# The last gate chunk of a feed-forward half and the split of the next weight block: a change of order on two engines

## The chip, the cores and the metric

One NeuronCore of one Trainium2 chip runs the whole program. The time is device microseconds (us) of one execution, as the median of the runs. TensorE (PE) multiplies, VectorE (DVE) and ScalarE (ACT) do everything elementwise, GpSimd (POOL) computes a few roots, and SyncE's queue (SP) starts the weight transfers.

## What is computed

Two transformer layers with adaptive normalization (feed-forward, a mixer, feed-forward each), then two hybrid layers and a final norm, on a context of 256 rows and a sequence of 256 rows, width 1024. The change concerns the feed-forward sublayers alone, of which there are four: ffn00, ffn01, ffn10 and ffn11 (layer, which of the two). The first three work on 512 columns (context and sequence), ffn11 on the 256 of the sequence alone, since nothing reads the context afterwards.

```python
D_MODEL = 1024; D_FF = 2816

def _ffn_sublayer(h, mod, g_pre, g_post, w_in, w_out):
    shift, scale, gate = mod
    u = _modulate(_rmsnorm(h, g_pre), shift, scale)
    a, b = jnp.split(u @ w_in, 2, axis=-1)
    y = (jax.nn.silu(a) * b) @ w_out
    return h + MACARON_W * gate * _rmsnorm(y, g_post)
```

## The kernel before, in words

Activations lie transposed: 128 features on the partitions, columns of the sequence along the free axis. Every large product is made of fp32 operands that are split in two parts of reduced precision, high and low, so that one step over 128 features is three matmuls: high by high, high by low, low by high (`product_step`, L915 to L917). Each operand therefore has two tiles: `uR` (normalized input) and `gR` (gated hidden values) with their parts 0 and 1, and the weights `wh` and `wl`.

**Weights.** They come as blocks of 128 x 2048 values or less, in two slots. SP starts a block's transfer into `wraw` as soon as the block two before it has been split (it waits for the semaphore `w_lo`, L671). ACT rounds the block into `wh` (`lead`, L1602), DVE subtracts to get `wl` (`rest`, L2096, or in two halves L2114) and then raises `w_lo`, which PE waits for at the start of the block. `lead` also waits until PE has done with the slot's old block. So the split of a block runs while PE works on the block before it.

**A feed-forward sublayer** is cut in two halves of the hidden width: 12 chunks of 128 and then 10. In each half a loop (two chunks to a turn) makes the gate chunks: PE makes a chunk's two products, a and b; ACT takes the silu of a (L1912) into `half`; DVE multiplies it by b (L2639); ACT then copies the product as `gR` high (L1916); DVE subtracts for `gR` low (L2644) and raises `g_ready`. After the loop comes the output projection of the half (`out_proj`): 8 weight blocks (`out0` to `out7` in this text), one for each 128 output features, each multiplied with all 12 (or 10) chunks of `gR`. The very first of them starts right after the last gate product, and waits for `g_ready` chunk by chunk, so only its last step needs the last gate chunk.

**Order of the work on ACT and DVE**, before. For each gate chunk ACT does: silu, `lead` of the block two ahead, copy to `gR` high. DVE does: multiply, `rest` of that block, subtract for `gR` low. The blocks two ahead of the last two gate blocks are out0 and out1. Each engine takes its instructions strictly in the order written; `do` also makes it wait for its own instruction before it signals others (the idle time that such a signal ends is listed as DVEq L2002 or ACTq L1542). In the first half's projection ACT copies each of the 8 products out of PSUM (L1922) and then leads the next block. In the second half DVE adds the products to `yT` (L2668), and the pieces of the norm that follows run beside it.

**Between sublayers.** The function `residual` ends a sublayer on DVE with a chain: variance, root on POOL (L1963), spread over the partitions by PE (L866), scaling, adding, normalizing (L2191, L2196, L2072, L2081). The next sublayer's block 1 is split inside this chain in two column halves (`rest_part`, L2114): the first half before the last wait for POOL's root (signal `w_half`), since PE's first step makes three products together, two of block 0 and the first of block 1. The second half and its `w_lo` come after the whole chain, except ahead of the sublayer na, where both halves stand in front.

**ada chunks.** ffn00, ffn01 and the second half of ffn10 carry a side product, one to a turn: PE L820, copied by ACT to `gs` (L1564, `ada_out`), then turned by PE (L830, `ada_turn`). In the loops the turn comes a turn later; after the loop of ffn10's second half PE does the last one at once, ahead of the output projection.

## Time and profile before

| | us |
|---|---|
| median of three runs | 2489.59 (2488.76, 2489.59, 2499.67) |
| the profiled execution, its own time | 2494.8 |
| its span, first to last instruction | 2492.9 |
| PE busy | 2341.6 (94%) |
| DVE busy | 1239.6 (50%) |
| ACT busy | 1022.9 (41%) |
| POOL busy | 33.5 (1%) |
| mean granted clock of TensorE | 0.968 |

PE is the engine that is nearly always busy. The time that a change of order can move is PE's idle time, so the rows to look for are those in which PE waits: each carries in brackets how long it had been idle and which engine's signal ended the idle time. PE's rows overlap, since matmuls are pipelined; the distance between two starts is the pace.

### The profile page before, as it was taken

What the parts mean: (1) busy time and instruction counts of PE and PEld (TensorE: products, weight loads), DVE (VectorE), ACT (ScalarE), POOL (GpSimd) and SP (SyncE); (2) the same over time, 40 slices, a digit from 0 to 9 for tenths busy, and PEclk for the clock granted to TensorE, in tenths of its full rate; (3) what the DMA queues carried; (4) which work ended last, traced back from release to release, by engine and by line L of the source; (5) the groups of instructions that cost most, each with busy time, mean ns of one, the idle gap of its engine ahead of it and who ended that gap; (6) DMA issues with size and microseconds to landing.
All of it is one profiled execution on the core that took longest, in us unless ns stands there. A gap on an engine that the chain in (4) does not pass through costs nothing.

```text
span 2492.9 us, 41414 instructions
## 1 busy us (share of the span) xinstructions
PE 2341.6 (94%) x15342; PEld 2007.9 (81%) x15342; DVE 1239.6 (50%) x1709; ACT 1022.9 (41%) x1459; POOL 33.5 (1%) x35
## 2 busy tenths in 40 slices
PE   6999999899898999998999999899789979998998
PEld 5888888777677888887888877777689979988997
DVE  4332335755656322337432336655564576856765
ACT  4332224543455332235322224543554455344543
POOL 0000000000000000000000000000000000000000
PEclk8999999999999999999999999999999999999999
DMA  9553553322214544542333643422245543214221
GB/s 305 186 177 93 170 175 94 114 90 85 85 35 135 157 142 139 168 131 72 103 87 106 193 138 95 113 79 69 68 135 169 160 139 112 69 54 138 85 69 52
DMA packets 396899, 298.16 MB, mean 120 GB/s; under 512 B 10846, under 2 KB 358756, under 8 KB 396644
## 3 DMA queue, kind: packets, MB, share of 16 engines
q1 hardware_dynamic: 363274, 231.12, 31.2%
q10 hardware_dynamic: 33498, 65.35, 7.3%
q8 instruction: 80, 1.31, 0.2%
q14 instruction: 47, 0.39, 0.1%
HBM read 295.38 MB, written 1.06 MB: 119 GB/s over the span
## 4 chain that ended last, share of the span: by engine, by line
PE 80%; DVE 10%; ACT 4%; issue 3%; DMA 1%; SPq 1%; DVEq 0%; POOL 0%; ACTq 0%; POOLq 0%
PE banks L915 23%; PE banks L916 22%; PE banks L917 22%; DVE wl L2096 3%; PE banks L1173 3%; PE banks L820 2%; ACT wh L1602 2%; DVE wl L2114 1%; PE banks L1024 1%; SPq L671 1%; PE banks L1045 1%; DMA scratch<-in_ada_w 1%; PE banks L1131 1%; PE banks L1031 0%; PE banks L1221 0%
## 5 line engine op out<-in xcount | busy, mean ns | idle before, releaser
L915 PE MATMUL banks<-uR,wh 128*128 128x512 f32 (+2 forms) x2368 | 835.7, 353 | 41.7 <-DVE uR L2081 25.7
L916 PE MATMUL banks<-uR,wh 128*128 128x512 f32 (+2 forms) x2368 | 821.2, 347 | 0.0
L917 PE MATMUL banks<-uR,wl 128*128 128x512 f32 (+2 forms) x2368 | 819.7, 346 | 0.0
L2096 DVE TENSOR_TENSOR wl<-wraw,wh 128x2048 fp32r<-128x2048 f32 (+2 forms) x214 | 453.1, 2117 | 428.0 <-ACTq L1542 423.2
L1602 ACT ACTIVATE wh<-wraw 128x2048 fp32r<-128x2048 f32 (+2 forms) x224 | 398.7, 1780 | 482.6 <-PE banks L917 450.7
L915 PEld LDWEIGHTS banks<-uR,wh 128*128 128x128 f32 (+1 forms) x2368 | 458.8, 194 | 105.0 <-issue 41.3
L917 PEld LDWEIGHTS banks<-uR,wl 128*128 128x128 f32 (+1 forms) x2368 | 458.1, 193 | 52.9
L916 PEld LDWEIGHTS banks<-uR,wh 128*128 128x128 f32 (+1 forms) x2368 | 458.8, 194 | 49.7 <-issue 0.5
L915 PE MATMUL banks<-gR,wh 128*128 128x512 f32 (+1 forms) x704 | 256.5, 364 | 4.6 <-DVEq L2002 4.5
L916 PE MATMUL banks<-gR,wh 128*128 128x512 f32 (+1 forms) x704 | 255.4, 363 | 0.0
L917 PE MATMUL banks<-gR,wl 128*128 128x512 f32 (+1 forms) x704 | 255.3, 363 | 0.0
L2639 DVE TENSOR_TENSOR half<-half,banks 128x512 f32<-128x512 f32 (+1 forms) x88 | 54.7, 622 | 400.7 <-PE banks L917 390.2
L915 PEld LDWEIGHTS banks<-gR,wh 128*128 128x128 f32 x704 | 132.9, 189 | 27.4 <-DVEq L2002 3.7
L917 PEld LDWEIGHTS banks<-gR,wl 128*128 128x128 f32 x704 | 132.9, 189 | 20.6
L916 PEld LDWEIGHTS banks<-gR,wh 128*128 128x128 f32 x704 | 132.9, 189 | 20.2
L1912 ACT ACTIVATE half<-banks 128x512 f32<-128x512 f32 (+1 forms) x88 | 47.9, 545 | 169.0 <-PE banks L917 140.6
L915 PE MATMUL banks<-wh,uR 128*128 128x256 f32 (+1 forms) x320 | 93.2, 291 | 2.2 <-DVEq L2002 2.2
L917 PE MATMUL banks<-wh,uR 128*128 128x256 f32 (+1 forms) x320 | 90.5, 283 | 0.0
L916 PE MATMUL banks<-wl,uR 128*128 128x256 f32 (+1 forms) x320 | 90.5, 283 | 0.0
L1922 ACT ACTIVATE yT<-banks 128x512 f32<-128x512 f32 (+1 forms) x32 | 17.4, 545 | 159.6 <-PE banks L917 159.6
L1593 ACT ACTIVATE uR<-yT,mod,coefA 128x256 fp32r<-128x256 f32 x88 | 52.2, 594 | 56.4 <-DVE yT L2072 56.3
L2644 DVE TENSOR_TENSOR gR<-half,gR 128x512 f32 (+1 forms) x88 | 55.1, 626 | 30.5 <-DVE wl L2096 30.5
(305 smaller groups left out, 2398.0 us busy)
## 6 DMA issues: line engine op xcount, KB each, us to landing
wraw<-in_ffn_w_in SPq DMA_DIRECT2D x176, 512.0 KB, 5.0
ada_buf<-in_ada_w ACTq DMA_DIRECT2D x27, 2048.0 KB, 8.3
wraw<-in_w_in SPq DMA_DIRECT2D x56, 512.0 KB, 4.5
wraw<-in_ffn_w_out SPq DMA_DIRECT2D x64, 384.0 KB, 4.1
wraw<-in_ffn_w_out SPq DMA_DIRECT2D x64, 320.0 KB, 3.7
wraw<-in_da_w_in SPq DMA_DIRECT2D x24, 512.0 KB, 4.5
wraw<-in_na_w_in SPq DMA_DIRECT2D x24, 512.0 KB, 4.4
yT<-in_ada_w ACTq DMA_DIRECT2D x4, 2048.0 KB, 8.4
```

What stands on the lines that cost most here:

```text
L671: sp.dma_start(dst, src).then_inc(w_in[s], 16)
L820: ins = mm(o[32 * j:32 * j + 32, 0:P], sc[:, k, :], w[:, k, j * P:j * P + P], start=(k == 0), stop=(k == DC - 1))
L915: mm(o, a[0], b[0], start=first, stop=False)
L916: mm(o, a[0], b[1], start=False, stop=False)
L917: return mm(o, a[1], b[0], start=False, stop=last)
L1173: ins = mm(o[:, h * P:h * P + P], a, b, start=(k == 0), stop=(k == len(parts) - 1))
L1593: A_(uR[:, 0, k, a], yT[:, k, a], ACT.Identity, **at_)
L1602: do(A_(wh[:, s, 0:n], wraw[:, s, 0:n], ACT.Copy), w_hi)
L1912: do(A_(half[:, s, 0:w], o[:, 0:w], ACT.Silu), silu_ready)
L2096: do(V.tensor_tensor(wl[:, s, 0:n], wraw[:, s, 0:n], wh[:, s, 0:n].bitcast(F32), ALU.subtract), w_lo)
L2639: do(V.tensor_tensor(half[:, s, 0:w], half[:, s, 0:w], o[:, 0:w], ALU.mult), free_a, free_b, gm_ready)
L2644: do(V.tensor_tensor(gR[:, 1, k, c0:T], half[:, s:s + 1, 0:w], gR[:, 0, k, c0:T].bitcast(F32), ALU.subtract), g_ready)
```

## The change

Three edits, all on ACT and DVE:

1. The last turn of each gate loop is written out after the loop, and in its second chunk, the last of the half, the `gR` work stands before the weight work: on ACT the copy, then `lead`; on DVE the subtraction for `gR` low, then `rest`. The block is out1 of the half. All other chunks keep their order. This concerns 8 places.
2. In the first half's output projection ACT leads the next block before it copies the product out of PSUM (32 places).
3. Ahead of ffn11, `residual` splits the second column half of block 1 right after the first, ahead of the wait for the root, and no longer after the chain.

```diff
@@ ScalarE
+                        def two_chunks(i, last):
                             ada_load(carries, n0, i)
                             for s in range(2):
...
-                                lead(s)
+                                if not (last and s):
+                                    lead(s)
                                 act.wait_ge(gm_ready, tl["gm"].up())
                                 do(A_(gR[:, 0, bass.ds(i * 2 + s, 1), c0:T], half[:, s:s + 1, 0:w], ACT.Copy), gh_ready)
+                                if last and s:
+                                    lead(s)
                             if carries:
                                 ada_out()
+
+                        with repeat(act, kc // 2 - 1, (gemm, 4), (own, 6 + len(ada)), (tl["g"], 2), (tl["gm"], 2), (tl["w0"], 32),
+                                    (tl["w1"], 32), (tl["split"], 2), *ada) as i:
+                            two_chunks(i, False)
+                        two_chunks(kc // 2 - 1, True)
                         if part == 0:
                             for b in range(DC):
                                 o, free = product()
+                                lead_next()
                                 do(A_(yT[:, b:b + 1, c0:T], o[:, 0:w].rearrange(one, a=1), ACT.Copy), free)
-                                lead_next()
@@ VectorE, residual
-                if to not in SUB or to == "na":
+                if to not in SUB or to in ("na", "ffn11"):
                     rest_part(b, 1, to in SUB, w_lo)
...
-                if to in SUB and to != "na":
+                if to in SUB and to not in ("na", "ffn11"):
                     rest_part(b, 1, True, w_lo)
@@ VectorE, gate chunks
-                                rest(s)
+                                if not (last and s):
+                                    rest(s)
                                 dve.wait_ge(gh_ready, tl["gh"].up())
                                 k = bass.ds(i * 2 + s, 1)
                                 do(V.tensor_tensor(gR[:, 1, k, c0:T], half[:, s:s + 1, 0:w],
                                                    gR[:, 0, k, c0:T].bitcast(F32), ALU.subtract), g_ready)
+                                if last and s:
+                                    rest(s)
```

ACT at the end of ffn11's first gate loop and the start of its output projection, before (L156 is the loop's end, L1916 the copy to `gR` high, L1602 the lead, first of out1, then of out2):

```order
L1912 ACTIVATE half<-banks 128x256
L1540 REGISTER_ALU
L1599 REGISTER_ALU
L1602 ACTIVATE wh<-wraw 128x2048
L1540 REGISTER_ALU
L1916 ISA
L1916 ACTIVATE gR<-half 128x256
L1540 REGISTER_ALU
L156 REGISTER_ALU
L156 COMPARE_AND_BRANCH
L1922 ACTIVATE yT<-banks 128x256
L1602 ACTIVATE wh<-wraw 128x1536
```

The same place after the change, from the silu of the loop's last chunk on (L1917 is now the copy to `gR` high, L1931 the copy out of PSUM):

```order
L1912 ACTIVATE half<-banks 128x256
L1917 ACTIVATE gR<-half 128x256
L1602 ACTIVATE wh<-wraw 128x2048
L1602 ACTIVATE wh<-wraw 128x1536
L1931 ACTIVATE yT<-banks 128x256
L1602 ACTIVATE wh<-wraw 128x1536
```

The copy of the last chunk has moved ahead of the 2048-wide lead, and each projection's lead ahead of its copy; DVE is reordered in the same manner (subtraction L2653, then L2104).

DVE ahead of ffn11, before: the end of the variance chain, the first column half of block 1, and the start of scaling.

```order
L2178 TENSOR_SCALAR stat<-stat 128x2
L2114 TENSOR_TENSOR wl<-wraw,wh 128x8x128
L2030 CAST rootR<-stat 128x2
L2031 TENSOR_TENSOR rootR<-stat,rootR 128x2
L2191 TENSOR_TENSOR yT<-yT,banks 128x256 x2
L2196 TENSOR_TENSOR hT<-hT,yT 128x256
```

The same place after the change:

```order
L2186 TENSOR_SCALAR stat<-stat 128x2
L2122 TENSOR_TENSOR wl<-wraw,wh 128x8x128 x2
L2038 CAST rootR<-stat 128x2
L2039 TENSOR_TENSOR rootR<-stat,rootR 128x2
L2199 TENSOR_TENSOR yT<-yT,banks 128x256 x2
L2204 TENSOR_TENSOR hT<-hT,yT 128x256
```

Two column halves now stand ahead of the cast that waits for the root, where one stood; the one behind the chain is gone.

ACT at the end of ffn10's second gate loop after the change (L1564 is `ada_out`, for which PE's turn L830 waits):

```order
L1912 ACTIVATE half<-banks 128x512
L1917 ACTIVATE gR<-half 128x512
L1602 ACTIVATE wh<-wraw 128x2048
L1564 ACTIVATE gs<-banks 128x128
L1602 ACTIVATE wh<-wraw 128x1280
L1937 ACTIVATE scratch<-yT 128x512
```

Before, the lead stood ahead of the copy; `ada_out` was and is behind both. PE's and SP's instructions are the same, in the same order, in both kernels.

## Rows read from the trace of the kernel before

**Rows 1.** The page: the span, and PE's line of busy time.

```profile
span 2492.9 us, 41414 instructions
PE 2341.6 (94%) x15342; PEld 2007.9 (81%) x15342; DVE 1239.6 (50%) x1709; ACT 1022.9 (41%) x1459; POOL 33.5 (1%) x35
```

**Rows 2.** Waits, 1805 to 2060 us: line, releaser: us in total, times, longest.

```profile
PE banks L915 <- DVEq L2002: 9.3, 5, 2.9
```

**Rows 3.** Timeline, ffn11, end of first half's gates: start, duration, instruction, [idle before <-releaser].

```profile
1888.71 1.92 ACT L1602 ACTIVATE wh<-wraw 128x2048 fp32r<-128x2048 f32 x1 [2.42 <-PE banks L917]
1888.80 0.42 DVE L2639 TENSOR_TENSOR half<-half,banks 128x256 f32<-128x256 f32 x1 [0.67 <-PE banks L917]
1890.70 2.29 DVE L2096 TENSOR_TENSOR wl<-wraw,wh 128x2048 fp32r<-128x2048 f32 x1 [1.48 <-ACTq L1542]
...
1893.38 0.42 DVE L2644 TENSOR_TENSOR gR<-half,gR 128x256 f32 x1 [0.39 <-DVE wl L2096]
1892.35 0.28 PE L917 MATMUL banks<-gR,wl 128*128 128x256 f32 x1
1893.92 0.39 PE L915 MATMUL banks<-gR,wh 128*128 128x256 f32 x1 [1.29 <-DVEq L2002]
```

**Rows 4.** Timeline, ffn11's first gates, on DVE and ACT.

```profile
1831.84 0.42 DVE L2639 TENSOR_TENSOR half<-half,banks 128x256 f32<-128x256 f32 x1 [0.40 <-DVE gR L2644]
...
1832.65 0.42 ACT L1916 ACTIVATE gR<-half 128x256 f32 x1 [0.96 <-DVEq L2002]
```

**Rows 5.** Timeline, ffn11, output projection of the first half.

```profile
1912.55 1.49 ACT L1602 ACTIVATE wh<-wraw 128x1536 fp32r<-128x1536 f32 x1 [0.18 <-ACT yT L1922]
1922.30 1.92 ACT L1602 ACTIVATE wh<-wraw 128x2048 fp32r<-128x2048 f32 x1 [1.29 <-DMA wraw<-in_ffn_w_in]
1926.78 0.38 PE L915 MATMUL banks<-uR,wh 128*128 128x256 f32 x1 [1.87 <-DVEq L2002]
```

**Rows 6.** Timeline, ffn11, output projection of the second half.

```profile
1991.35 0.39 PE L915 MATMUL banks<-gR,wh 128*128 128x256 f32 x1 [2.01 <-DVEq L2002]
2000.76 1.27 ACT L1602 ACTIVATE wh<-wraw 128x1280 fp32r<-128x1280 f32 x1 [2.18 <-DMA wraw<-in_ffn_w_out]
2003.97 0.36 PE L915 MATMUL banks<-gR,wh 128*128 128x256 f32 x1 [1.21 <-DVEq L2002]
```

**Rows 7.** Timeline, from the chain ahead of ffn11 to its third weight block.

```profile
1808.60 0.70 POOL L1963 TENSOR_TENSOR stat<-stat,lams 128x2 f32<-128x2 f32 x1 [1.94 <-DVEq L2002]
1808.61 1.26 DVE L2114 TENSOR_TENSOR wl<-wraw,wh 128x1024 fp32r<-128x1024 f32 x1
1810.09 0.17 DVE L2030 CAST rootR<-stat 128x2 fp32r<-128x2 f32 x1 [0.22 <-DVE wl L2114]
1813.95 0.55 PE L915 MATMUL banks<-uR,wh 128*128 128x256 f32 x1 [2.27 <-DVE uR L2081]
1822.77 1.22 DVE L2114 TENSOR_TENSOR wl<-wraw,wh 128x1024 fp32r<-128x1024 f32 x1
1830.82 0.38 PE L915 MATMUL banks<-uR,wh 128*128 128x256 f32 x1 [2.93 <-DVEq L2002]
```

**Rows 8.** Timeline, ffn10, end of the first half's gates (512 columns).

```profile
1305.59 0.69 DVE L2639 TENSOR_TENSOR half<-half,banks 128x512 f32<-128x512 f32 x1 [5.61 <-PE banks L917]
...
1313.66 0.60 ACT L1922 ACTIVATE yT<-banks 128x512 f32<-128x512 f32 x1 [5.39 <-PE banks L917]
```

**Rows 9.** Timeline, ffn10, end of the second half's gates.

```profile
1488.80 0.69 DVE L2639 TENSOR_TENSOR half<-half,banks 128x512 f32<-128x512 f32 x1 [5.21 <-PE banks L917]
1491.72 0.28 ACT L1564 ACTIVATE gs<-banks 128x128 f32<-128x128 f32 x1 [0.25 <-ACT gR L1916]
1492.10 0.33 PE L830 MATMUL banks<-cst,gs 128*128 128x128 f32 x1 [1.54 <-ACTq L1542]
```

**Rows 10.** Stretches: us, busy (instructions) of PE, PEld, DVE, ACT, POOL, PEclk, DMA share, GB/s.

```profile
1900.00:1925.00 25.00, 24.91 (x207) 24.63 (x205) 9.50 (x6) 10.78 (x12) 0.00 (x0) 1.00 0.71 206
1928.00:1932.00 4.00, 4.00 (x23) 4.00 (x23) 2.29 (x1) 1.29 (x2) 0.00 (x0) 0.57 0.94 264
```

More of the change, by code:

```diff
@@ L1904, in _ @@
                         ada, n0 = [(tl["ada"], 1)] if carries else [], tl["ada"].n
-                        with repeat(act, kc // 2, (gemm, 4), (own, 6 + len(ada)), (tl["g"], 2), (tl["gm"], 2), (tl["w0"], 32),
-                                    (tl["w1"], 32), (tl["split"], 2), *ada) as i:
+                        def two_chunks(i, last):
                             ada_load(carries, n0, i)
@@ L2630, in _, with two_chunks @@
                         ada = [(tl["ada"], 1)] if ada_parts(st)[part] else []
-                        with repeat(dve, kc // 2, (gemm, 4), (own, 6 + len(ada)), (tl["silu"], 2), (tl["gh"], 2),
-                                    (tl["split"], 2), *ada) as i:
+                        def two_chunks(i, last):
                             for s in range(2):
@@ L2645, in _ @@
                                                    gR[:, 0, k, c0:T].bitcast(F32), ALU.subtract), g_ready)
+                                if last and s:
+                                    rest(s)
+                        with repeat(dve, kc // 2 - 1, (gemm, 4), (own, 6 + len(ada)), (tl["silu"], 2), (tl["gh"], 2),
+                                    (tl["split"], 2), *ada) as i:
+                            two_chunks(i, False)
+                        two_chunks(kc // 2 - 1, True)
                         if part == 0:
```

## The prediction

> **What bounds the kernel now.** I read the page first: PE is busy 94% of a span of 2492.9 us, DVE and ACT half of it [rows 1]. So only PE's idle time can be given back by a change of order, 2492.9 - 2341.6 = 151 us in all. Next came the waits of PE by stretch, and then the timeline at the places that the diff touches. In ffn11, from 1805 to 2060 us, PE waited for a signal of DVE before a product step five times, 9.3 us together [rows 2]. They are: 2.93 us for the third weight block [rows 7], 1.29 us for the last gate chunk of the first half [rows 3], 1.87 us for the first gate block of the second half [rows 5], 2.01 us for the last gate chunk of the second half and 1.21 us for a later block of that projection [rows 6]. In the three sublayers of 512 columns PE's steps last twice as long and the same places show no wait, but for one: the last turn of the ada product in ffn10, 1.54 us [rows 9].
>
> **Edit 1, the last gate chunk first, in ffn11's first half.** What goes: the wait for `g_ready`, 1.29 us. What comes is read off the same rows, with the instructions in their new order. The multiplication ends at 1888.80 + 0.42 = 1889.22 [rows 3]. Its signal took 0.39 us to start ACT's copy elsewhere (1832.26 to 1832.65 [rows 4]), so the copy runs from 1889.61 to 1890.03 (0.42). The lead follows an ACT copy by 0.18 us [rows 5]: 1890.21 to 1892.13 (1.92). DVE began its subtraction 0.07 us after the lead (1890.63 to 1890.70): 1892.20 to 1894.49 (2.29), and PE hears of DVE after 0.12 us (1893.80 to 1893.92): 1894.61 [all rows 3]. PE's pace is 25.00 / 207 = 0.12 us a matmul [rows 10]. Without the wait it runs on from 1892.35 for three more matmuls and wants out1 at 1892.83; before, it reached out1 at 1893.92 plus three, about 1894.38. So **the wait does not go, it moves by one step**: from `g_ready`, 1.29 us, to `w_lo` of out1, 1.8 us, and PE starts out1 at 1894.61 against 1894.38, +0.2 us. The 0.39 us holds the loop's register instructions, which the written-out turn doesn't have; halved, the result is 0. I take +0.1, bounds 0 and +0.4. The gain that the edit seems to promise is excluded: lead and subtraction alone need 4.2 us after 1890.03.
>
> **The same in the second half.** PE's wait was 2.01 us there and is about 2.5 us for out1 now, +0.1 us by the same steps. But DVE and ACT also take up the projection's next blocks earlier, since the lead of out2 no longer waits for PE. The later wait of 1.21 us hangs on a transfer that landed at 2000.76, after ACT had waited 2.18 us for it [rows 6]; the transfer starts when out2 is split. By the new order that is some 0.7 us earlier, while the transfer ahead of it (out3) starts 1.5 us later. After that DVE's chain is back to back to the end of the sublayer, so what is won there stays. Bounds: -1.2 (the wait goes) and +0.4 (the transfer is pushed back); I take -0.5 for the half, which is the 0.7 less half of the 0.4.
>
> **Edit 1 in the six wide halves.** The tightest is ffn10's first, which has no ada product between. The multiplication ends at 1306.28; then 0.39 signal, 0.60 copy (as L1922), 0.18, 1.92, 0.07, 2.29, 0.12: out1 is ready at 1311.85. PE wants it when out0 is done, about 0.2 us before ACT's copy of it at 1313.66 [rows 8]: 1.6 us of cover. The others have the ada product in between, about 2 us (PE's idle time before 1492.10 began at 1490.56, its last gate product ended near 1488.6 [rows 9]); the second halves' group is a sixth shorter, 1.4 us of 8.2. I cost them at 0; the work that hides them is PE's out0.
>
> **Edit 1 at ffn10's last turn.** PE turns the ada product right after the loop, behind ACT's `ada_out`, which is behind lead and copy. Before, lead, copy and `ada_out` began 0.09 us before the multiplication (as in rows 3), at 1488.71, and `ada_out` started at 1491.72, 3.01 us on. Now the copy has to wait for the multiplication, 1488.80 + 0.69 + 0.39 = 1489.88, and `ada_out` starts at 1492.89: the wait of 1.54 us becomes up to 2.7. With the shorter signal it is 1.0 more. **+1.0 us**, bounds +0.8 and +1.2.
>
> **Edit 2, lead before copy.** ACT's copy (0.38) and the gap behind it (0.18) leave the chain lead, subtraction, transfer [rows 5]: 0.56 us. Where PE bounds the blocks it is worth nothing, which is everywhere at 512 columns. It counts once: ffn11's first gate block of the second half, for whose transfer ACT waited 1.29 us and PE 1.87 us. The transfer starts when out6 is split, hence 0.56 us earlier. **-0.56 us**, bounds -1.2 and 0. Each PSUM bank is free 1.5 to 1.9 us later; its next user is four products on, so that costs nothing.
>
> **Edit 3, the second column half in front.** DVE's first half runs from 1808.61 to 1809.87; POOL's root was ready at 1809.30, and the cast that needs it started at 1810.09 with DVE as its releaser [rows 7]. DVE is the last to arrive, so a second half in front adds its whole length, 1.22 to 1.26 us, to the chain. Behind it are queued scaling, addition and normalization of all eight feature blocks, hence PE's first step of ffn11 (1813.95). What it takes away was hidden: at 1822.77 to 1823.99 PE was busy with its 72 first matmuls until after 1824.4. The 2.93 us wait that follows hangs on the third block, whose lead needs PE to be done with block 0, and stays. SP gets to load the fourth block earlier, which nobody awaits. **+1.24 us**, bounds 0 (if the root is the later one after all) and +1.3.
>
> Here a page speaks of the same place. POOL's root ran from 1808.60 to 1809.30, 0.70 us, together with DVE's half split, which took 1.26 us against 1.22 us without POOL [rows 7]; neither held the other up. The Trainium skill, "SBUF — State Buffer", section "Who interferes with whom", says that a DVE instruction with two SBUF inputs and a GpSimd instruction that reads SBUF exclude each other for their whole length. By that rule the root could be held until both halves are done; the rows speak against it.
>
> **The sum.** +0.1 - 0.5 + 1.0 - 0.56 + 1.24 = +1.3 us. On the profiled execution that is 2494.8 to 2496.1; it was 5 us above the median of the runs, and the difference applies as it is: 2489.59 + 1.3 = **2490.9 us**. This is no change: about 0.5%, 12 us, is what a measurement of this kernel can tell.
>
> **Rivals.**
>
> *The gains come without the costs* (17%). The root is late enough to hide edit 3, the wait of 1.21 goes whole, and the lower clock behind the 1.87 us wait goes with it: from 1928 to 1932 the granted clock was 0.57, that is mostly 1.2 GHz, and PE made 23 matmuls in 4 us, where the pace before gives 33 [rows 10], 1.2 to 1.7 us lost. 0.1 - 1.1 + 1.0 - 0.56 - 1.7 = -2.3: 2487.3.
>
> *Waits that grew bring the lower clock* (15%). The same row the other way: three waits are longer now, 2.6 us in ffn10 and 1.8 and 2.5 us in ffn11. Against it: after the wait of 1.29 us the clock was 1.00 from 1900 to 1925 [rows 10]. If each is followed by such a stretch: 1.3 + 3 x 1.5 = +5.8, 2495.4.
>
> *The cover is gone* (4%), the slower side. If out1 comes later than PE wants it in the wide halves too, each of eight loses what it is late. It decides at 1.6 us beyond the working above; with a transfer or a signal late by twice that, 8 x 1.6 = 13 us: 2503.
>
> *Root and split exclude each other* (4%). POOL would start after the second half, at 1811.1, and end 0.70 us later; the cast starts at 1812.0 and not 1811.3. +2.0: 2491.6. It is what the skill's page named above gives.
>
> *Nothing moves* (10%). The small terms cancel: 2489.6.
>
> **How the numbers follow.** The forecast has 50%, its own range 2489 to 2493. The range of 8 in 10 takes in the faster rival with its bound of edit 2, and the clock rival, and two to three us of the runs' own scatter on each side: 2485 to 2498. Faster by over 0.5%: 3%; only the cover's rival is slower by as much, with a stray median 5%; within: 92%.
>
> **What would show it.** Right: PE's wait for `g_ready` at the two ends of ffn11's gates gone, and a wait of 1.5 to 2.5 us 36 (or 30) matmuls after the start of out0; PE's turn in ffn10 with 2.3 to 2.7 us of idle time; the cast of ffn11's root 1.2 us later with DVE as releaser; ACT's wait for the gate block's transfer as long as before but 0.5 us earlier. Wrong: no wait at out1, a cast released by POOL, any wait at the six wide halves' out1, or new stretches at half the clock.

## The result: 9 us slower, outside the forecast range

| | kernel before | changed kernel |
|---|---|---|
| median | 2495.31 us (11 runs) | 2504.3 us (11 runs, one of them 6940 us) |
| ratio | | 1.0038, interval 1.0027 to 1.0049 |
| profiled execution | 2494.8 us, granted clock 0.968 | 2506.36 us, granted clock 0.963 |

The forecast was 2490.9 us, a difference of +1.3 us, in a range of 2485 to 2498. Measured was a difference of about +9.5 us (0.38%, interval 6.7 to 12.2). It is still under the 0.5% called "no change", but it is a loss beyond its interval, and the time lies outside the range. (The one run of 6940 us is left out of the ratio; without it the median is 2504.27.) Part of the miss has nothing to do with the change: the 2489.59 us from which the sum started was the median of three runs, and all later medians of the kernel before were 2495.1 to 2496.8 us.

The page of the changed kernel, its span and its busy times:

```profile
span 2504.5 us, 41127 instructions
PE 2354.2 (94%) x15342; PEld 2017.5 (81%) x15342; DVE 1238.8 (49%) x1709; ACT 1019.0 (41%) x1456; POOL 33.4 (1%) x35
```

Against [rows 1] the span is 11.6 us longer, PE is busy 12.6 us longer with the same 15342 instructions, and the other engines do what they did. In this pair of executions PE's idle time did not grow; the same matmuls took longer, at a lower clock. But one pair does not show what the change does. A second execution of the changed kernel, then one of the kernel before, were profiled later:

```profile
span 2500.6 us, 41127 instructions
PE 2346.9 (94%) x15342; PEld 2012.7 (80%) x15342; DVE 1239.6 (50%) x1709; ACT 1020.7 (41%) x1456; POOL 33.4 (1%) x35
```

```profile
span 2492.4 us, 41414 instructions
PE 2346.2 (94%) x15342; PEld 2011.7 (81%) x15342; DVE 1239.5 (50%) x1709; ACT 1022.7 (41%) x1459; POOL 33.5 (1%) x35
```

Here the span is 8.2 us longer and PE is busy only 0.7 us longer: 7.5 us are idle time. So the split into idle time and slower matmuls differs from pair to pair, and the loss has to be looked for place by place.

The timeline of the changed kernel, PE at the places that the prediction worked out (start, length, instruction, in brackets the idle time and who ended it):

```profile
1494.29 0.33 PE L830 MATMUL banks<-cst,gs 128*128 128x128 f32 x1 [2.45 <-ACTq L1542]
1815.16 1.11 PE L866 MATMUL banks<-identR,rootR 128*128 128x128 f32 x4 [4.10 <-DVEq L2010]
1834.97 0.38 PE L915 MATMUL banks<-uR,wh 128*128 128x256 f32 x1 [2.92 <-DVEq L2010]
1900.10 0.38 PE L915 MATMUL banks<-gR,wh 128*128 128x256 f32 x1 [1.47 <-DVEq L2010]
1909.89 0.39 PE L915 MATMUL banks<-gR,wh 128*128 128x256 f32 x1 [0.89 <-DVEq L2010]
1932.99 0.38 PE L915 MATMUL banks<-uR,wh 128*128 128x256 f32 x1 [1.25 <-DVEq L2010]
1996.64 0.58 PE L915 MATMUL banks<-gR,wh 128*128 128x256 f32 x1 [2.19 <-DVEq L2010]
```

The first row answers to [rows 9]: the wait for the ada turn is 2.45 us, was 1.54. The third is the block of [rows 7], 2.92 after 2.93. The fourth stands for the wait of [rows 3], now at out1. The sixth answers to [rows 5], 1.25 after 1.87, and the seventh to [rows 6].

Behind the ada turn the stretches show what the waits' list cannot (us, busy time and count of PE, PEld, DVE, ACT and POOL, PEclk, DMA share, GB/s):

```profile
1493.00:1494.50 1.50, 0.21 (x1) 0.14 (x1) 0.69 (x1) 1.01 (x2) 0.00 (x0) 1.00 0.00 0
1494.50:1498.50 4.00, 3.91 (x11) 3.01 (x11) 2.29 (x5) 0.00 (x0) 0.00 (x0) 0.57 0.18 52
1498.50:1503.00 4.50, 4.50 (x22) 3.70 (x21) 0.00 (x0) 0.00 (x0) 0.00 (x0) 1.00 0.34 99
```

In the middle row PE works without a gap and makes 11 matmuls in 4.0 us, where the row behind it has 22 in 4.5 us: the clock was at its level of 1.2 GHz nearly throughout, 0.43 x 4.0 = 1.7 us lost. Neither trace of the kernel before has such a stretch there.

### The profile page after: what moved, and what is told of

It is laid out like the page before. It is cut to its first block, busy times and chain, and to the rows that moved or that the text cites. A ratio compares the mean times of both kernels' runs of the same rounds, so it can differ in the third digit from the quotient of the medians.

```text
span 2504.5 us, 41127 instructions
## 1 busy us (share of the span) xinstructions
PE 2354.2 (94%) x15342; PEld 2017.5 (81%) x15342; DVE 1238.8 (49%) x1709; ACT 1019.0 (41%) x1456; POOL 33.4 (1%) x35
## 3 DMA queue, kind: packets, MB, share of 16 engines
q8 instruction: 80, 1.31, 0.2%
## 4 chain that ended last, share of the span: by engine, by line
PE 79%; DVE 10%; ACT 4%; issue 3%; DMA 2%; SPq 1%; DVEq 0%; POOL 0%; ACTq 0%; POOLq 0%
PE banks L915 22%; PE banks L916 22%; PE banks L917 22%; DVE wl L2104 3%; PE banks L820 2%; PE banks L1173 2%; ACT wh L1602 2%; DVE wl L2122 1%; SPq L671 1%; PE banks L1024 1%; PE banks L1045 1%; PE banks L856 1%; ACT uR L1593 1%; DMA scratch<-in_ada_w 1%; ACT yT L1594 1%
## 5 line engine op out<-in xcount | busy, mean ns | idle before, releaser
L2104 DVE TENSOR_TENSOR wl<-wraw,wh 128x2048 fp32r<-128x2048 f32 (+2 forms) x214 | 453.0, 2117 | 419.8 <-ACTq L1542 414.9
L1602 ACT ACTIVATE wh<-wraw 128x2048 fp32r<-128x2048 f32 (+2 forms) x224 | 398.7, 1780 | 602.4 <-PE banks L917 563.7
L916 PEld LDWEIGHTS banks<-uR,wh 128*128 128x128 f32 (+1 forms) x2368 | 460.6, 195 | 49.6 <-issue 0.5
L1917 ACT ACTIVATE gR<-half 128x512 f32 (+3 forms) x88 | 51.0, 579 | 60.5 <-DVEq L2010 43.3
L2653 DVE TENSOR_TENSOR gR<-half,gR 128x512 f32 (+3 forms) x88 | 55.0, 625 | 33.6 <-DVE wl L2104 24.9
```

Of the source, the lines that this page charges most:

```text
L916: mm(o, a[0], b[1], start=False, stop=False)
L1602: do(A_(wh[:, s, 0:n], wraw[:, s, 0:n], ACT.Copy), w_hi)
L1917: do(A_(gR[:, 0, bass.ds(i * 2 + s, 1), c0:T], half[:, s:s + 1, 0:w], ACT.Copy), gh_ready)
L2104: do(V.tensor_tensor(wl[:, s, 0:n], wraw[:, s, 0:n], wh[:, s, 0:n].bitcast(F32), ALU.subtract), w_lo)
L2653: do(V.tensor_tensor(gR[:, 1, k, c0:T], half[:, s:s + 1, 0:w], gR[:, 0, k, c0:T].bitcast(F32), ALU.subtract), g_ready)
```

## The experiments

All were timed in five rounds beside the kernel before, on the same chip. Differences are the ratio less one times 2495.5 us, with their interval. One thing about their size first: the kernel before, timed as if it were a changed one (`before_again`, below), came out at +1.5 us (-1.2 to +4.2). A single difference under 3 us means little; weight lies on pairs that differ by one edit, and on the length of one stage in the traces, which repeats to 0.5 us.

The theories: **order** (the loss is the sum of longer waits, found place by place), **turn** (the longer wait at the ada turn, with the low clock that it brings, is most of it), **clock anywhere** (any shift of the work changes where the low stretches fall, whatever the edit).

### The three edits alone, and two together

**Edit 3 alone:**

```
-                if to not in SUB or to == "na":
+                if to not in SUB or to in ("na", "ffn11"):
```

> Only the third edit: both column halves of ffn11's second block stand in front of the cast that waits for the root. Theory A (order alone): the cast starts 1.2 us later with DVE as releaser, PE's 2.93 us wait for the third block stays, and the time is the kernel before's +1.2 to 1.3 us. Theory B (the rest of the +9 us of all three edits together is TensorE's granted clock, set off by waits that grew or moved): the order costs +1.3 us and the shift of everything behind it changes where half-clock stretches fall, so the time is +1 to +4 us and the profile shows other half-clock stretches behind 1805 us than before.

Measured: 2497.53 us, +2.7 us (-0.5 to +6.0), which both theories allow.

**Edit 1 alone** (the last gate chunk's two operations ahead of lead and rest, eight places):

```
-                                lead(s)
+                                if not (last and s):
+                                    lead(s)
                                 act.wait_ge(gm_ready, tl["gm"].up())
...
+                                if last and s:
+                                    lead(s)
```

> Only the first edit: the last chunk of each half is made ahead of the block's split, on ACT and DVE. Theory A (order alone): +1.0 us at ffn10's last ada turn, about +0.1 at each end of ffn11's gates, and up to -0.5 behind the second: +0.7 to +1.2 us in all. Theory B (clock): the turn's wait of 2.4 us in place of 1.5 is followed by a stretch at half the clock between 1490 and 1500 us, which costs 1.6 us more, and the waits for out1 in ffn11 can add one: +3 to +6 us, which would make this edit the largest part of the +9 us.

Measured: 2501.72 us, +6.2 us (3.5 to 9.0). Order alone falls.

**Edit 2 alone:**

```
                                 o, free = product()
+                                lead_next()
                                 do(A_(yT[:, b:b + 1, c0:T], o[:, 0:w].rearrange(one, a=1), ACT.Copy), free)
-                                lead_next()
```

> Only the second edit: in the first half's projection ACT leads the next block before it copies. Theory A (order alone): -0.56 us, PE's wait of 1.87 us for the first gate block of ffn11's second half becomes 1.3 us. Theory B (clock): the shorter wait also takes away the half-clock stretch of 1928 to 1932 us, worth 1.2 to 1.7 us more: -2.2 us. No part of the +9 us by either.

Measured: 2494.49 us, -0.2 us (-3.5 to +3.0). The interval takes in both theories.

**Edits 1 and 2:**

> The first and the second edit without the third. Theory A (order alone, terms add): the changed kernel less 1.2 us, that is about +8 us against the kernel before if the +9 us of all three are terms of the order. Theory B (clock): the sum of e2 and e3 as measured within 1 us, and the third edit accounts for what is left of the +9 us.

Measured: 2500.61 us, +6.7 us (4.0 to 9.5), 0.7 more than the sum of the two alone, as theory B had it; 8 is inside the interval too.

What follows: edits 2 and 3 agree with their forecasts of -0.56 and +1.24 us within their intervals. Edit 1 was forecast at +0.6 us in all and is most of the loss.

### Edit 1 place by place

**The written-out turn with the old order** (edit 1's loops one turn shorter, the last turn behind them, no operation moved):

```
+                        tail = False
+
+                        def two_chunks(i, last):
...
-                                if not (last and s):
+                                if not (tail and last and s):
                                     lead(s)
```

> Both two-chunk loops run one turn less and their last turn is written out behind them, as in edit 1, but with the old order: the lead and the rest stand ahead of gR's copy and subtraction everywhere. The computation is whole. Edit 1 alone measured +6.5 us. Theory 'order': that cost comes from where the last chunk's two operations stand, so the written-out turn alone gives 0 (within 1 us of the kernel before). Theory 'code': the written-out turn brings other instruction loads or branches on ACT and DVE, and most of the 6.5 us is seen here too: +3 to +6 us.

Measured: 2497.32 us, +1.5 us (-1.0 to +4.0), between the two theories. Most of edit 1's price is not in the code's form. A small part is. At the norm ahead of ffn01, about 764 us into the span, PE waited 2.65 or 2.66 us in every kernel with written-out turns, 2.29 to 2.31 us in every other. The DVE timeline shows where the 0.36 us come in, first without and then with written-out turns:

```profile
756.99 0.16 DVE L2173 TENSOR_TENSOR stat<-stat,banks 128x8 f32<-128x8 f32 x1
757.29 0.16 DVE L2174 TENSOR_TENSOR stat<-stat 128x4 f32<-128x4 f32 x1
```

```profile
760.58 0.16 DVE L2183 TENSOR_TENSOR stat<-stat,banks 128x8 f32<-128x8 f32 x1
761.24 0.16 DVE L2184 TENSOR_TENSOR stat<-stat 128x4 f32<-128x4 f32 x1 [0.50 <-DVE stat L2183]
```

The second operation waits for nothing but the first, by the same kind of wait, and starts 0.66 us after it, not 0.30. At this place only the position of the instructions in DVE's program differs. Why that costs 0.36 us was not tested.

**Edit 1 only at ffn10's last turn:** `tail = st == "ffn10" and part == 1`.

> Edit 1 at one place of eight: the last two-chunk turn of ffn10's second half, where the last ada turn stands behind it; the loops are written out as in edit 1 everywhere. The computation is whole. Theory 'turn': TensorE's wait for the ada turn grows from 1.54 to about 2.45 us (0.9 us) and the 5 us behind it come at the low clock now (some 2.5 us), so +2.5 to +4 us, about half of edit 1's 6.5. Theory 'spread': edit 1's cost is made of eight small ones, so +0.9 us here. Theory 'clock anywhere': the time goes with the mean granted clock, which any small shift changes, and then this gives as much as edit 1 whole, +5 to +7 us.

Measured: 2502.16 us, +5.2 us (3.0 to 7.7). Theory "spread" falls. The middle lies above the range of "turn" and in that of "clock anywhere"; the interval takes in both.

**Edit 1 only in ffn11:** `tail = st == "ffn11"`.

> Edit 1 at the two places of ffn11 alone (the narrow feed-forward); the loops are written out as in edit 1 everywhere. The computation is whole. Theory 'turn': 0 to +0.5 us in the places themselves (a wait of 1.29 us replaced by one of about 1.5, the later one of 1.21 gone), so within 1 us of the kernel before. Theory 'clock anywhere': other positions of the low-clock stretches behind it, +3 to +6 us.

Measured: 2501.08 us, +4.2 us (1.7 to 6.7). A miss for "turn", by which it is neutral: it costs nearly as much as the turn, and the two together are more than edit 1 whole. It is in the range of "clock anywhere".

**Edit 1 whole, the ada row's copy ahead of the last cast:**

```
                                 if last and s:
+                                    if carries:
+                                        ada_out()
                                     lead(s)
-                            if carries:
+                            if carries and not last:
                                 ada_out()
```

> Edit 1 whole, with one difference: in the written-out last turn of each loop that carries an ada product, ACT makes the ada row's copy ahead of the last weight block's cast, not behind it. The computation is whole. TensorE then waits at ffn10's last ada turn for gR's copy (0.63 us) and the row's copy (0.28 us) and no cast: about 0.5 us where edit 1 has 2.45 and the kernel before 1.54. Theory 'turn': this takes the turn's whole price off edit 1's +6.5 us and 1 us more, so +2 to +3.5 us against the kernel before. Theory 'spread' or 'clock anywhere': 1.9 us less than edit 1 at most, +4.6 us or more.

Measured: 2499.62 us, +3.0 us (-0.2 to +6.2), 3.2 less than edit 1 whole, as "turn" had it.

### The wait at the turn and the clock behind it

**Old order, the wait made longer** (written-out turns; ACT copies the ada row three times at ffn10's last turn):

```
+                for _ in range(again):
+                    do(A_(adarow, o[:, 0:P], ACT.Copy))
                 do(A_(adarow, o[:, 0:P], ACT.Copy), ada_rows, *free)
```

> The old order everywhere with the last turns written out (the kernel that measured +1.5 us), and at ffn10's last ada turn ACT copies the ada row three times instead of once, so that TensorE waits two copies longer there (2 x about 0.46 us: 1.37 to about 2.3 us, nearly edit 1's 2.45). Nothing of the order is changed, the computation is whole. Theory 'longer wait at the turn': the whole price of edit 1 at this place (+5.2 us against the kernel before, +3.7 against the written-out turns) comes from the 0.9 us and the low clock it brings in behind it, so this gives +4 to +6 us. Theory 'order': the price is elsewhere in the moved operations, and this gives the written-out turns' +1.5 and 0.9, about +2.4 us. Theory 'noise of the comparison': +1 to +3.

Measured: 2498.05 us, +3.0 us (0.5 to 5.5). The wait came out at 1.98 us, not 2.3. By time this lies nearer to "order" (+2.4) than to "longer wait" (+4 to +6) and decides nothing; its trace, below, does.

**Old order, the wait made shorter** (only the last turn of ffn10's second half: gR's copy and `ada_out` ahead of the cast):

> The old order with the last turns written out, and at one place, the last two-chunk turn of ffn10's second half, gR's copy and the ada row's copy both ahead of the last cast on ACT. The computation is whole. TensorE's wait at the last ada turn falls from 1.37 to about 0.45 us. Theory 'longer wait at the turn', read backwards: the wait's 0.9 us and any low clock behind it go, so -1 us or less against the kernel before (0.5 to -4). Theory 'order' or 'code': +1.5 less 0.9, about +0.6 us.

Measured: 2497.04 us, +0.7 us (-1.5 to +3.0). That is the figure of "order" or "code", and the interval does not exclude the other.

**The turn behind the first product of the out-projection** (TensorE alone), in the kernel before:

```
-                        if st == "ffn10" and part == 1:
-                            ada_turn()
...
                                       for k in range(kc)]).then_inc(gemm_full, 1)
+                            if first and turn:
+                                ada_turn()
```

> The kernel before with one change on TensorE: ffn10's last ada turn (a transpose) stands behind the first product of the out-projection, not ahead of it. ACT and DVE keep their order, the computation is whole. ACT's row copy is done long before that product ends, so the wait of 1.54 us goes and nothing takes its place (the last chunk's g_ready comes some 7 us ahead of the product's last step). Theory 'the turn's wait and the low clock it may bring': -1.5 us, and up to 1.7 more in the runs that had a low stretch there, so -1.5 to -2.5 us. Theory 'clock decides and waits do not': within 1 us of the kernel before.

Measured: 2494.82 us, +0.7 us (-2.5 to +4.0): what "clock decides and waits do not" said. By time no gain is seen.

**The same in the changed kernel:**

> The changed kernel with the same move of the last ada turn. The computation is whole. It removes the 2.45 us wait and, if the low stretch of 3.5 to 4 us behind it (1.7 us of work lost, in every profile with a wait of 1.98 us or more) comes from that wait, this too: -4.1 us against the changed kernel, +4 us against the kernel before. Theory 'clock decides and waits do not': +6 us or more.

Measured: 2498.94 us, +5.0 us (2.5 to 7.5), 4.5 less than the changed kernel, as the wait and its low stretch had it (-4.1).

The traces settle this stage. It is bounded by two waits that no edit touches, those of PE (L866, which spreads a norm's root over the partitions) ahead of ffn10 and behind it. In the changed kernel, then in the kernel before (second trace), the written-out turns with the old order, the longer wait, the shorter one, and the late turn:

```profile
1168.10 1.97 PE L866 MATMUL banks<-identR,rootR 128*128 128x128 f32 x8 [3.67 <-DVEq L2010]
1562.97 1.97 PE L866 MATMUL banks<-identR,rootR 128*128 128x128 f32 x8 [5.04 <-DVEq L2010]
```

```profile
1162.82 1.54 PE L866 MATMUL banks<-identR,rootR 128*128 128x128 f32 x6 [3.67 <-DVEq L2002]
1488.09 0.33 PE L830 MATMUL banks<-cst,gs 128*128 128x128 f32 x1 [1.54 <-ACTq L1542]
1555.12 1.97 PE L866 MATMUL banks<-identR,rootR 128*128 128x128 f32 x8 [5.04 <-DVEq L2002]
```

```profile
1166.78 1.97 PE L866 MATMUL banks<-identR,rootR 128*128 128x128 f32 x8 [3.67 <-DVEq L2012]
1491.89 0.33 PE L830 MATMUL banks<-cst,gs 128*128 128x128 f32 x1 [1.37 <-ACTq L1542]
1558.94 1.32 PE L866 MATMUL banks<-identR,rootR 128*128 128x128 f32 x5 [5.05 <-DVEq L2012]
```

```profile
1167.39 1.97 PE L866 MATMUL banks<-identR,rootR 128*128 128x128 f32 x8 [3.68 <-DVEq L2014]
1493.10 0.33 PE L830 MATMUL banks<-cst,gs 128*128 128x128 f32 x1 [1.98 <-ACTq L1542]
1561.79 1.97 PE L866 MATMUL banks<-identR,rootR 128*128 128x128 f32 x8 [5.04 <-DVEq L2014]
```

```profile
1164.79 1.66 PE L866 MATMUL banks<-identR,rootR 128*128 128x128 f32 x8 [3.68 <-DVEq L2013]
1489.22 0.33 PE L830 MATMUL banks<-cst,gs 128*128 128x128 f32 x1 [0.44 <-ACTq L1542]
1556.31 1.97 PE L866 MATMUL banks<-identR,rootR 128*128 128x128 f32 x8 [5.05 <-DVEq L2013]
```

```profile
1164.38 1.97 PE L866 MATMUL banks<-identR,rootR 128*128 128x128 f32 x8 [3.67 <-DVEq L2007]
1494.95 0.27 PE L830 MATMUL banks<-cst,gs 128*128 128x128 f32 x1
1554.84 1.97 PE L866 MATMUL banks<-identR,rootR 128*128 128x128 f32 x8 [5.04 <-DVEq L2007]
```

First row from last, the stage's length:

| wait at the turn | kernels | stage, us | low clock behind the turn |
|---|---|---|---|
| none (late turn) | 5 | 390.5 to 390.7 | none |
| 0.44 | 2 | 391.3, 391.5 | none |
| 1.36 to 1.54, clock full | 5 | 392.2 to 392.7 | none |
| 1.54 (edit 2 alone) | 1 | 393.9 | 0.57 over 4.0 us |
| 1.98 | 1 | 394.4 | 0.51 over 3.5 us |
| 2.45 | 6 | 394.8 to 395.2 | in each |

Two rows behind the last column, for the longer wait and for the written-out turns:

```profile
1494.00:1497.50 3.50, 3.50 (x10) 2.68 (x10) 1.08 (x5) 0.00 (x0) 0.00 (x0) 0.51 0.68 187
```

```profile
1492.30:1500.00 7.70, 7.70 (x34) 6.39 (x35) 2.59 (x7) 0.63 (x1) 0.00 (x0) 1.00 0.29 85
```

The stage's length is the wait plus, where a low stretch follows, 1.7 us: 390.5 + 2.45 + 1.7 = 394.7. A low stretch followed in all seven traces with 1.98 us or more, and in one of the thirteen with less. With the operations in the old order and nothing but the wait longer it came too, and with the operations moved but the turn late it did not. So **at this place the wait brings it, not the order**: in the stage, edit 1 costs 0.9 + 1.7 = 2.6 us. The Trainium skill, "TensorE: Matmul & The Clock Gate", section "What's actually happening", says that a gate sets the clock by how busy TensorE has recently been, and that one kernel starts with a different number of matmuls at the low clock from run to run. The table agrees with the first half; of the second, what the traces show is that a wait of the same 1.54 us had a low stretch behind it in one trace of four.

It is not a rule for every wait of that length. In ffn11 PE waits 2.92 us for the third weight block, in all twenty traces, and in ten of them the clock stays full behind it. The changed order's wait for out1 in ffn11's second half, 2.19 us, has a low stretch behind it in three traces of seven; the wait of 1.77 or 2.01 us that it replaces has one in eight of thirteen. Behind the 2.93 us in the kernel before, behind 2.20 us in the changed kernel's second trace, and behind 2.19 us in its first, the granted clock (the third number from the end) is 1.00, 1.00 and 0.66:

```profile
1831.00:1836.00 5.00, 5.00 (x43) 5.00 (x43) 3.56 (x4) 2.78 (x4) 0.00 (x0) 1.00 0.78 213
```

```profile
1993.60:1998.60 5.00, 5.00 (x42) 5.00 (x43) 2.69 (x4) 1.89 (x4) 0.00 (x0) 1.00 0.70 201
```

```profile
1996.60:2001.60 5.00, 4.96 (x29) 4.96 (x30) 2.34 (x3) 1.34 (x3) 0.00 (x0) 0.66 0.66 197
```

### ffn11, and what adds up

**The changed kernel once more, and the kernel before once more:**

> The changed kernel once more, unchanged, beside these runs. If the earlier comparison holds, +8 to +10 us, and the profile has the long low-clock stretches in both hybrid layers (14 and 17.5 us long) and a low stretch behind ffn10's last ada turn. If the comparison itself wanders from call to call, +5 to +7 us, and the profile may have the short stretches (7 us each).

Measured: 2503.16 us, +9.2 us (6.0 to 12.5). The loss repeats.

> The kernel before once more as if it were a changed one: the size of the difference that means nothing. 0 within 1 us. If the low-clock stretches are a property of the kernel, its profile has them where the first one has (7 us from 2085 and from 2314 us); if they are a property of the run, it may have the long ones.

Measured: 2495.14 us, +1.5 us (-1.2 to +4.2). Its profile, unlike the first one, has long low stretches in the hybrid layers, as the changed kernel's, so a single trace of them says nothing about a kernel. The first of them, in the kernel before, in its second trace, and in the changed kernel:

```profile
2085.00:2092.00 7.00, 7.00 (x24) 4.93 (x23) 1.79 (x6) 3.79 (x5) 0.00 (x0) 0.51 0.48 152
```

```profile
2080.00:2094.00 14.00, 14.00 (x56) 11.93 (x56) 6.28 (x12) 5.49 (x8) 1.63 (x1) 0.51 0.32 88
```

```profile
2092.00:2106.00 14.00, 14.00 (x56) 11.93 (x57) 6.26 (x12) 5.49 (x8) 1.64 (x1) 0.51 0.31 87
```

**The changed kernel without edit 1 in ffn11:** `tail = st != "ffn11"`.

> The changed kernel without edit 1 in ffn11 (old order there, the last turns written out); edits 2 and 3 and edit 1's other six places stay. The computation is whole. Theory 'ffn11's places cost too' (edit 1 there alone gave +4.2 us, +2.7 against the written-out turns; its four waits in ffn11 sum to 5.8 to 6.1 us against 5.4): -2 to -3 us against the changed kernel, +5 to +6.5 against the kernel before. Theory 'ffn11 is neutral, as predicted, and its +2.7 was scatter': +8 us as the changed kernel.

Measured: 2496.04 us, +2.5 us (0.2 to 4.7), 7 less than the changed kernel, where 2 to 3 less was forecast. Theory "ffn11 is neutral" falls a second time, from the other side.

What the traces show of it is less. PE's waits for DVE in ffn11's gates and projections, first in the changed kernel's second trace, then in the kernel before's:

```profile
1897.08 0.39 PE L915 MATMUL banks<-gR,wh 128*128 128x256 f32 x1 [1.48 <-DVEq L2010]
1906.83 0.39 PE L915 MATMUL banks<-gR,wh 128*128 128x256 f32 x1 [0.86 <-DVEq L2010]
1929.85 0.38 PE L915 MATMUL banks<-uR,wh 128*128 128x256 f32 x1 [1.17 <-DVEq L2010]
1993.50 0.39 PE L915 MATMUL banks<-gR,wh 128*128 128x256 f32 x1 [2.20 <-DVEq L2010]
```

```profile
1888.78 0.38 PE L915 MATMUL banks<-gR,wh 128*128 128x256 f32 x1 [1.29 <-DVEq L2002]
1921.21 0.38 PE L915 MATMUL banks<-uR,wh 128*128 128x256 f32 x1 [1.20 <-DVEq L2002]
1984.31 0.41 PE L915 MATMUL banks<-gR,wh 128*128 128x256 f32 x1 [2.01 <-DVEq L2002]
```

5.71 us against 4.50. Over all traces these waits sum to 5.0 to 6.4 us, 5.9 in the mean, in the seven with edit 1 in ffn11, and to 4.1 to 6.4, 5.1 in the mean, in the thirteen without. Low clock adds nothing to that: from the third weight block to the end of the sublayer it costs 2.0 us in the mean with edit 1 in ffn11 and 2.1 without. Nor does what follows: the hybrid layers with the final norm take 461.3 us in the mean with it and 460.6 without, each between 457 and 466. The second row of the changed kernel is a wait that the forecast did not have; six of the seven traces have it (0.58 to 1.00 us), and none of the thirteen. Its cause stands on ACT and DVE of the changed kernel:

```profile
1895.71 1.92 ACT L1602 ACTIVATE wh<-wraw 128x2048 fp32r<-128x2048 f32 x1 [0.18 <-ACT gR L1917]
1897.70 2.29 DVE L2104 TENSOR_TENSOR wl<-wraw,wh 128x2048 fp32r<-128x2048 f32 x1 [1.67 <-ACTq L1542]
1906.45 1.49 ACT L1602 ACTIVATE wh<-wraw 128x1536 fp32r<-128x1536 f32 x1 [5.75 <-DMA wraw<-in_ffn_w_out]
```

out1's split ends at 1899.99, 1.4 us after PE wants it, and out3's transfer starts when the split is done; it lands 6.46 us later, and lead and split follow. In both traces of the kernel before ACT has no wait for a transfer in these blocks. The moved split makes the block after next late.

**Both parts out: no edit 1 in ffn11, and the late turn:**

> The changed kernel with both suspected parts removed: edit 1 not in ffn11, and the last ada turn behind the first product of the out-projection. The computation is whole. By the parts: the changed kernel without ffn11's places measured +2.5 us against the kernel before, and the late turn takes 4.4 us off the stage where it stands, so -1.9 us. If the parts don't add up because a shorter stage is paid back by the clock later, 0 to +3 us.

Measured: 2493.91 us, -1.2 us (-4.0 to +1.5); -1.9 was the sum of the parts. The loss is gone, so its carriers are these two places; how ffn11's carries as much as it does is another matter.

**The kernel before with the late turn and edit 2, twice:**

> The kernel before with the late ada turn and edit 2 (the lead ahead of the copy in the first half's projection, -0.8 us alone). The computation is whole. If both add up: -2.3 us, with a profile that has neither wait at the turn nor the low stretch behind it. If edit 2 gives nothing and the clock takes back the rest: -1 to +1 us.

Measured: 2494.44 us, -2.0 us (-5.2 to +1.2).

> The kernel before with the late ada turn and edit 2, once more, to tell -2 us (0.9992, interval 0.9979 to 1.0005) from none: -1.8 us by the stage (1.54 us of wait gone, and 0.3 of low clock), -2.6 with edit 2's own. If the clock pays it back, within 1 us of the kernel before.

Measured: 2497.29 us, +1.0 us (-1.7 to +3.7). No gain that can be measured: the stage is 1.6 to 2.1 us shorter in every trace of a late turn than in the kernel before, and the end of the kernel does not show it. No kernel here beats the kernel before.

A fit over 18 comparisons gives each part one price, such that the prices of the parts in a kernel come as near as possible to its time (least squares; the longer-wait kernel is left out, and the turn is not counted where it is late or short). It leaves about 1.1 us unexplained per comparison: edit 1 at the turn +4.4 us (standard error 0.8), in ffn11 +5.3 (0.8), at its five other places -3.4 (1.0), written-out turns +0.5 (0.6), edit 2 -0.5 (0.7), edit 3 +2.5 (0.7), late turn +0.2 (0.7). The errors are somewhat too small, since comparisons share runs of the kernel before. In the stages where the five other places stand the traces show no difference, so the -3.4 is more likely a sign that turn and ffn11 cost less together than each alone.

**What stays open.** Of the 9 us the traces locate 2.6 at the turn, 0.4 in the norm, 1.1 to 1.4 in edit 3's chain and about 1 in ffn11: some 5. The rest lies in stages whose order is unchanged, and not in the same ones each time: in the first pair of traces 6.3 us of the 11.6 lie in the hybrid layers, in the second pair 0.1 of the 8.2. Over all runs but the one of 6940 us the mean granted clock is 0.9674 for the kernel before (172 runs) and 0.9655 for the changed one (18 runs); (1 - clock) times the time is 81.4 and 86.4 us, so up to 5 of the 9 us go with the clock, of which the turn's stretch is 1.7. That is an upper bound, since about 20 of these us fall on PE's idle time, where a low clock costs nothing. So "turn" holds in its stage and covers less than a third of the loss, "order" covers about as much again, and "clock anywhere" is not excluded for the rest: the turn alone, ffn11 alone and the late turn in the kernel before came out in its ranges, though the late turn in the changed kernel (+5.0 where it had 6 or more) and the ada row's copy moved ahead (+3.0 where it had 4.6 or more) did not. Why edit 1 in ffn11 costs 4 to 7 us by time and about 1 us in the traces could not be told with one trace per kernel.

## Why the prediction was wrong, point by point

- **Baseline.** The median of three runs was taken as the kernel's time. It was 5.7 us below the 2495.3 of the longer series, and the profiled execution at 2494.8, called "5 us above the median", was the typical one. Of the 13.4 us between forecast and result 5.7 are this.
- **Edit 1 at the turn.** The wait was forecast at 2.3 to 2.7 us and was 2.45; +1.0 against +0.91. Right. What failed is that the term ended there: the low clock behind it, 1.7 us in all six traces with this wait, was kept out of the sum and given 15% as a rival. The evidence against it was a wait of 1.29 us with full clock behind [rows 10], which says nothing about a wait of 2.45. That it came in each trace could not be read from the rows of before, where waits of 2.01 and 2.93 us in ffn11 have full clock behind them.
- **Edit 1 in ffn11, first half.** "The wait does not go, it moves by one step" is right: 1.47 us at out1, 1.8 forecast, and against the 1.29 that went +0.2, as worked out. The step that failed is the transfer behind it: out3's was not followed in this half, and its wait of 0.89 us was missed.
- **Edit 1 in ffn11, second half.** 2.19 us at out1, about 2.5 forecast. The credit of 0.5 us hung on a wait of 1.21 us for a transfer [rows 6]. It stands in six of the thirteen traces with the old order in ffn11 (0.77 to 1.21 us), not in the second one of the kernel before, and in none of the seven with the new order. So the edit seems to take it away, as said, but there is only about half as often something to take. By time ffn11's two places cost +5.3 us in the fit where -0.4 was forecast: the largest miss. The traces explain about 1 us of it, the later wait in the first half most of all; the rest stays open.
- **The six wide halves.** Right: no wait at out1 in any.
- **Written-out turns.** Not costed; 0.36 us in one norm.
- **Edit 2.** The gate block's wait fell from 1.87 to 1.25, -0.62 against -0.56; -0.5 us by time. The second trace of the kernel before has 1.20 in the same place, so the single pair of rows does not prove it; over all traces the wait is 1.31 us in the mean in the nine with edit 2 and 1.73 in the eleven without, -0.42. Right in size.
- **Edit 3.** DVE is the last to arrive, as said, and the spread's wait grew from 2.73 to 4.10 us, +1.37 against +1.24; in the second pair from 2.74 to 3.87, +1.13. Right. By time +2.5 in the fit (standard error 0.7), the difference being unexplained. The changed kernel:

```profile
1811.83 0.70 POOL L1971 TENSOR_TENSOR stat<-stat,lams 128x2 f32<-128x2 f32 x1 [1.93 <-DVEq L2010]
1811.84 2.63 DVE L2122 TENSOR_TENSOR wl<-wraw,wh 128x1024 fp32r<-128x1024 f32 x2
1814.69 0.17 DVE L2038 CAST rootR<-stat 128x2 fp32r<-128x2 f32 x1 [0.22 <-DVE wl L2122]
```

- **Rivals.** POOL's root is shown from 1811.83 to 1812.53, beside two DVE operations with two SBUF inputs, and the cast behind them was released by DVE and not by POOL. So "root and split exclude each other" falls here. The rule of the Trainium skill, "SBUF — State Buffer", section "Who interferes with whom", shows no effect in these rows, as in [rows 7]; but POOL works on two elements per partition there and its times are rough, so they are a weak test of it. "The cover is gone" falls too. "Waits that grew bring the lower clock" is the one that happened, at the turn in every trace and behind ffn11's out1 in three of seven, and its 2495.4 was itself short by the baseline: by its +5.8 and the right baseline it gives 2501.1.

## What to carry to other kernels

Where TensorE is busy 94% of the time, a wait is worth its length and what the clock does behind it. Give the low stretch a place in the sum of a wait that grows to some 2 us, as here, and a chance, as the same wait can have it in one trace and not in another (here 0.9 us at the turn cost 2.6, and waits of 2.2 and 2.9 us in ffn11 had a stretch behind them in about half of the traces). Book no gain beyond its length, and perhaps not even that, on a wait that is merely shortened. Follow each moved split to the transfer that it releases and on to the block after next. The smaller the effect, the more runs the baseline needs: the median of three lay 5.7 us off. Ask of every row that carries a term whether a second trace of the same kernel has it too.

## What was not expected of the hardware

- At the ada turn a wait of 1.98 to 2.45 us was followed by about 3.5 us at the 1.2 GHz level in seven of seven traces, one of 0.44 to 1.54 us in one of eight, and no wait in none of five. In ffn11 a wait of 2.92 us was followed by such a stretch in ten of twenty traces, and one of 2.19 us in three of seven.
- Unchanged code differs by low clock alone: the second hybrid layer and the rest behind it took 218.9 to 222.9 us, and a low stretch was 7 us long in one execution and 14 us in another of the same kernel at the same place. The runs of one kernel lay 5 to 17 us apart, and their times go with their mean clock (the correlation over the 172 runs of the kernel before is -0.76).
- Two dependent DVE operations, the second on 128x4 elements, start 0.30 us apart, and 0.66 us at one place when other code ahead of them is written out.
